# The recurrent layer's input strips computed as high and low parts in three products, with a changed order on VectorE

## The reference

```
xs = proj + (prev - proj) * mu                 # proj = rmsnorm(h) @ rwkv_w_in, 256 x 2816
r, k, v, wl, al, gl = jnp.split(xs, offs, axis=-1)
w = -jax.nn.softplus(-(w0 + jnp.tanh(wl) @ w2)) - 0.5
decay = jnp.exp(-jnp.exp(w.astype(jnp.float32)))
a = jax.nn.sigmoid(a0 + al @ a2)
g = jax.nn.sigmoid(gl) @ g2
kk = (k * k_k).reshape(B, S, H, N).astype(jnp.float32)
kk = kk * lax.rsqrt(jnp.maximum(jnp.sum(kk * kk, axis=-1, keepdims=True), 1e-24))
k = k * (1.0 + (a - 1.0) * k_a)
...
s = jnp.einsum('bshd,bmhd->bhsm', q, mem_k).astype(jnp.float32) * (HEAD_DIM ** -0.5)
p = jax.nn.softmax(s, axis=-1)
```

## Time and profile before

| | us |
|---|---|
| median of 3 runs | 764.37 (762.6 to 765.59) |
| the profiled execution: its own time | 763.08 |
| the profiled execution: span of its trace | 761.4 |
| PE busy in the span | 721.2 (95%) |
| DVE busy | 443.9 (58%) |
| ACT busy | 393.1 (52%) |
| first strip's first matmul to the first chunk matmul | 363.56 to 463.19 |

### The profile page before, as it was taken

How to read it: one execution, slowest core, us unless ns; L and a number is a source line. 1 busy time by engine, 2 the same in 40 slices (tenths; PEclk the granted TensorE clock), 3 DMA queues, 4 the chain that set the end, 5 groups by cost and what they waited for, 6 DMA issues and landing times.

```text
span 761.4 us, 14999 instructions
## 1 busy us (share of the span) xinstructions
PE 721.2 (95%) x6453; PEld 619.7 (81%) x6453; DVE 443.9 (58%) x645; ACT 393.1 (52%) x655; POOL 106.6 (14%) x163
## 2 busy tenths in 40 slices
PE   4999998999999999999999998998799999999997
PEld 4789975688888888888888877997678888888885
DVE  3778787646865675532243547553557757656523
ACT  5744766547655555532465535543258554556311
POOL 8120066700000000000300054700000000000000
PEclk9999989999999999999999999999999999999999
DMA  8846710008665565553844331000028565655511
GB/s 308 314 143 203 268 56 2 2 0 262 209 204 183 185 203 168 218 169 111 278 129 158 111 111 59 4 5 4 3 87 273 183 205 169 207 177 191 196 56 55
DMA packets 78276, 111.70 MB, mean 147 GB/s; under 512 B 2124, under 2 KB 64738, under 8 KB 78210
## 3 DMA queue, kind: packets, MB, share of 16 engines
q1 hardware_dynamic: 77090, 107.67, 42.4%
q0 software_dynamic: 976, 3.04, 1.2%
q10 hardware_dynamic: 144, 0.04, 0.0%
HBM read 109.68 MB, written 1.05 MB: 145 GB/s over the span
## 4 chain that ended last, share of the span: by engine, by line
PE 87%; DVE 5%; ACT 4%; issue 2%; DMA 1%; POOL 0%; DVEq 0%; SPq 0%; ACTq 0%; POOLq 0%
PE ps L1060 20%; PE ps L746 10%; PE ps L748 10%; PE ps L747 10%; PE ps L1063 10%; PE ps L1048 8%; PE ps L1225 5%; PE ps L1235 3%; PE ps L780 2%; PE ps L866 2%; PE ps L889 2%; PE ps L915 2%; DVE w_lo L1895 2%; DMA hn<-mem 1%; ACT w_hi L1422 1%
## 5 line engine op out<-in xcount | busy, mean ns | idle before, releaser
L1895 DVE TENSOR_TENSOR w_lo<-w_raw,w_hi 128x2048 fp32r<-128x2048 f32 (+2 forms) x90 | 202.2, 2260 | 84.5 <-ACT w_hi L1422 84.5
L1060 PE MATMUL ps<-x_hi_lo,w_hi 128*128 128x512 f32 x640 | 201.2, 396 | 0.0
L1422 ACT ACTIVATE w_hi<-w_raw 128x2048 fp32r<-128x2048 f32 (+2 forms) x90 | 168.0, 1886 | 39.6 <-PE ps L748 38.2
L1063 PEld LDWEIGHTS ps<-x_hi_lo,w_lo 128*128 128x128 f32 x640 | 120.2, 188 | 28.4
L1063 PE MATMUL ps<-x_hi_lo,w_lo 128*128 128x256 f32 x640 | 125.7, 278 | 0.0
L1060 PEld LDWEIGHTS ps<-x_hi_lo,w_hi 128*128 128x128 f32 x640 | 97.4, 189 | 0.0
L746 PE MATMUL ps<-w_hi,x_hi_lo 128*128 128x512 f32 (+3 forms) x208 | 74.0, 356 | 5.3 <-DVE x_hi_lo L2123 3.4
L748 PE MATMUL ps<-w_hi,x_hi_lo 128*128 128x512 f32 (+3 forms) x208 | 71.9, 346 | 0.0
L747 PE MATMUL ps<-w_lo,x_hi_lo 128*128 128x512 f32 (+3 forms) x208 | 71.9, 346 | 0.0
L746 PE MATMUL ps<-w_hi,hidden_hi 128*128 128x512 f32 x176 | 68.6, 390 | 0.0
L747 PE MATMUL ps<-w_lo,hidden_hi 128*128 128x512 f32 x176 | 68.5, 389 | 0.0
(11 more groups left out here) (367 smaller groups left out, 984.8 us busy)
## 6 DMA issues: line engine op xcount, KB each, us to landing
w_raw<-w_ffn_in SPq DMA_DIRECT2D x44, 1024.0 KB, 5.1
w_raw<-w_ffn_out SPq DMA_DIRECT2D x22, 1024.0 KB, 4.9
w_raw<-rwkv_w_in SPq DMA_DIRECT2D x11, 1024.0 KB, 5.3
w_raw<-w_out SPq DMA_DIRECT2D x8, 1024.0 KB, 4.9
w_raw<-nsa_w_in SPq DMA_DIRECT2D x6, 1024.0 KB, 14.7
w_raw<-w_mem_kv SPq DMA_DIRECT2D x2, 1024.0 KB, 8.9
w_raw<-nsa_cmp_k_w SPq DMA_DIRECT2D x2, 1024.0 KB, 5.5
w_raw<-nsa_cmp_v_w SPq DMA_DIRECT2D x2, 1024.0 KB, 5.5
```

Of the source, the lines that this page charges most:

```text
L1060: pe.matmul(psum[:, bank + j, :], kt_of(w_hi, i, k)[:, cols[j]], xx[:, k, :, :].rearrange("p c n -> p (c n)"), start=k == 0, stop=False)
L1063: ins = pe.matmul(psum[:, bank + j, 0:SEQ], kt_of(w_lo, i, k)[:, cols[j]], xh[:, k, :], start=False, stop=k == KD - 1)
L1422: act.activation(w_hi[:, i % SPL, 0:size(i)], raw[:, i % RAW, 0:size(i)], ACT.Copy).then_inc(hi_done, 1)
L1895: dve.tensor_tensor(w_lo[:, i % RAW, 0:size(i)], raw[:, i % RAW, 0:size(i)], w_hi[:, i % SPL, 0:size(i)], ALU.subtract).then_inc(lo_done, 1)
```

## The change

All 11 strips are split into high and low parts like every other piece: ACT and DVE each get 11 more instructions of 128x2048, `x_rwkv` goes, and `join(1)` writes `x_hi_lo` as the other joins do. In `feature_strip` and `tok_strip` the one float32 product becomes three of fp32r. Counters that skipped the strips (`whole`, `split_no`) go. On DVE the lower bound of the key norms moves from step 5 to step 4, ahead of that step's `shift`; the scaled `kkT` and `aT` stand ahead of `shift(6)`; `split_to` loses the exception on ACT and on DVE alike; the twelve `a_rT` come in two halves of six around the first row maxima; the bonus terms and the scaled keys come later; ACT makes no split in step 6 and the last one in step 7.

```diff
             def tok_strip(m, t, part, i):
-                if whole(i):
-                    pe.wait_ge(landed[i % RAW], land_value[i])
-                else:
-                    pe.wait_ge(lo_done, split_no(i) + 1)
+                pe.wait_ge(lo_done, i + 1)
                 for k in range(KD):
-                    if whole(i):
-                        if part == 0 and k % 2 == 0:
-                            pe.wait_ge((j_hi, j_lo)[k // 2 % 2], tile_base(m, t) + k // 4 + 1)
-                        ins = pe.matmul(psum[:, turn_bank(m, t) + part, 0:FC], xf[:, k, tile(t)], raw_kt(i, k),
-                                        start=k == 0, stop=k == KD - 1)
-                        continue
...
             def feature_strip(i, bank, between=None):
-                pe.wait_ge(landed[i % RAW], land_value[i])
+                pe.wait_ge(lo_done, i + 1)
                 for j in range(2):
                     c = slice(P * j, P * j + P)
                     for k in range(KD):
-                        ins = pe.matmul(psum[:, bank, j * SEQ:(j + 1) * SEQ], raw_kt(i, k)[:, c], xf[:, k, :],
-                                        start=k == 0, stop=k == KD - 1)
+                        ins = three(psum[:, bank, j * SEQ:(j + 1) * SEQ], kt_of(w_hi, i, k)[:, c], kt_of(w_lo, i, k)[:, c],
+                                    xh[:, k, :], xl[:, k, :], start=k == 0, stop=k == KD - 1)
...
             def split_to(n):
                 for i in range(split[0], min(n, NPIECES)):
-                    if whole(i):
-                        continue
...
-                if 2 <= q <= MQ - 1:
+                if 2 <= q < MQ - 1:
                     split_to(first["rwkv"] + q + 3 + AHEAD)
+                if q == MQ:
+                    split_to(first["rwkv"] + MQ + 2 + AHEAD)
...
-            def rate_factors():
+            def rate_factors(fs):
                 dve.wait_ge(ex_ok, 2)
                 dve.wait_ge(shifted, 7)
-                for f in range(FT):
+                for f in fs:
...
-                split_to(first["rwkv"] + q + 3 + AHEAD)
+                if q < MQ - 1:
+                    split_to(first["rwkv"] + q + 3 + AHEAD)
+                if q == 4:
+                    for j in range(FT // 2):
+                        dve.wait_ge(ss_mm, j + 1)
+                        dve.tensor_scalar(eP_sq[:, 2 * j:2 * j + 2, :], psum[:, j, :].rearrange("p (j n) -> p j n", j=2), 1e-24, None,
+                                          ALU.max).then_inc(ss_ev, 1)
+                if q == 6:
+                    dve.wait_ge(ss_rt, 1)
+                    link(dve.tensor_tensor(kkT[:], kkT[:], eP_sq[:], ALU.mult))
+                    link(dve.tensor_tensor(aT[:], aT[:], kkT[:], ALU.mult))
                 if q not in (0, 3):
                     shift(q)
...
+            rate_factors(range(FT // 2))
             maxima(1, 0)
-            bonus_terms()
+            rate_factors(range(FT // 2, FT))
             maxima(1, 1)
             factors(1, 0)
-            shift(MQ + 1)
-            scaled_keys()
+            split_to(first["rwkv"] + MQ + 2 + AHEAD)
             maxima(1, 2)
             factors(1, 1)
-            shift(MQ + 2)
+            shift(MQ + 1)
+            bonus_terms()
             maxima(1, 3)
             factors(1, 2)
             probs_out(1, 1)
+            shift(MQ + 2)
             factors(1, 3)
+            scaled_keys()
```

More of the change, by code:

```diff
@@ L170, in trunk @@
         xh, xl = xx[:, :, 0, :], xx[:, :, 1, :]
-        xf = at(o_x, "x_rwkv", [P, KD, SEQ])
         o_hn = base[0]
@@ L390, in kt_of @@
             return buf[:, i % (RAW if buf is w_lo else SPL), k * n:(k + 1) * n]
-        N_STRIPS = len(RWKV_ORDER)
-        def whole(i):
-            return first["rwkv"] <= i < first["rwkv"] + N_STRIPS
-        def split_no(i):
-            return i if i < first["rwkv"] else i - N_STRIPS
-        def raw_kt(i, k):
-            n = pieces[i].shape[2]
-            return raw[:, i % RAW, k * n:(k + 1) * n]
         def tile_base(m, t):
-            return (0, 8, 12)[m] + (2 if m == 1 else 4) * t
+            return 4 * (TT * m + t)
         land_value, count = [], [0] * RAW
@@ L1023, in full_gemm @@
                     if t == 0:
-                        pe.wait_ge(lo_done, split_no(i0 + j) + 1)
+                        pe.wait_ge(lo_done, i0 + j + 1)
                         if j < n_ready:
@@ L1275, in _ @@
             pe.wait_ge(bo_ev, 3)
-            pe.wait_ge(ar_ok, 1)
+            pe.wait_ge(ar_ok, 2)
             pe.wait_ge(bk_ok, 1)
@@ L1580, in tile_hi @@
                     col = NORM_COL[m + 2] + k
-                    if m == 1:
-                        if k // 2 % 2 == 0:
-                            ins = act.activation(xf[:, k, tile(t)], quarter(m, t, k), ACT.Copy, scale=colA[:, col:col + 1])
-                            if k % 2:
-                                ins.then_inc(j_hi, 1)
-                        continue
                     ins = act.activation(xh[:, k, tile(t)], quarter(m, t, k), ACT.Copy, scale=colA[:, col:col + 1])
@@ L1891, in split_to @@
                 for i in range(split[0], min(n, NPIECES)):
-                    if whole(i):
-                        continue
-                    dve.wait_ge(hi_done, split_no(i) + 1)
+                    dve.wait_ge(hi_done, i + 1)
                     dve.tensor_tensor(w_lo[:, i % RAW, 0:size(i)], raw[:, i % RAW, 0:size(i)], w_hi[:, i % SPL, 0:size(i)],
@@ L2112, in tile_lo @@
                     col = NORM_COL[m + 2] + k
-                    if m == 1:
-                        if k % 4 == 2:
-                            dve.wait_ge(j_tp, 2 * n + k // 4 + 1)
-                        if k // 2 % 2:
-                            ins = dve.tensor_scalar(xf[:, k, tile(t)], quarter(m, t, k), colA[:, col:col + 1], None, ALU.mult)
-                            if k % 2:
-                                ins.then_inc(j_lo, 1)
-                        continue
                     if k % 2 == 0:
@@ L2284, in bonus_terms @@
             def bonus_terms():
-                dve.wait_ge(ar_ok, 1)
+                dve.wait_ge(ar_ok, 2)
                 for f in range(FT):
@@ L2325, in _ @@
                     link(dve.tensor_tensor(k_T[:].rearrange(flat), vT[:].rearrange(flat), k_T[:].rearrange(flat), ALU.mult))
-                if q == 5:
-                    for j in range(FT // 2):
-                        dve.wait_ge(ss_mm, j + 1)
-                        dve.tensor_scalar(eP_sq[:, 2 * j:2 * j + 2, :], psum[:, j, :].rearrange("p (j n) -> p j n", j=2), 1e-24, None,
-                                          ALU.max).then_inc(ss_ev, 1)
-                if q == 6:
-                    dve.wait_ge(ss_rt, 1)
-                    link(dve.tensor_tensor(kkT[:], kkT[:], eP_sq[:], ALU.mult))
-                    link(dve.tensor_tensor(aT[:], aT[:], kkT[:], ALU.mult))
-                    rate_factors()
+            rate_factors(range(FT // 2))
             maxima(1, 0)
-            bonus_terms()
+            rate_factors(range(FT // 2, FT))
             maxima(1, 1)
             factors(1, 0)
-            shift(MQ + 1)
-            scaled_keys()
+            split_to(first["rwkv"] + MQ + 2 + AHEAD)
             maxima(1, 2)
             factors(1, 1)
-            shift(MQ + 2)
+            shift(MQ + 1)
+            bonus_terms()
             maxima(1, 3)
```

1 line of the change is left out of this document (removed).

## The result

| | us, median | lowest to highest | executions |
|---|---|---|---|
| before | 764.98 | 762.60 to 769.73 | 4 |
| after | 753.09 | 752.75 to 757.05 | 4 |

The ratio is 0.985, with a 95% interval of 0.982 to 0.988. Two later groups gave 0.986 (0.983 to 0.989; 753.94 against 765.27) and 0.986 (0.984 to 0.988; 753.35 against 764.67). The profiled execution of the changed kernel took 752.97 us, with a span of 751.2. The forecast was 755.3, with a range of 752.0 to 760.5.

What follows compares the result with a forecast made beforehand. PE alone was taken to bound the strips. Cheaper products save 12.65 us, less 0.64, 1.4 and 2.3 us at three waits: 8.3 us less, giving 754.8 or 756.1; forecast 755.3 us, range 752.0 to 760.5.

Steps and rivals of the forecast that it cites:

- The product: Each strip's 48 fp32r products start 0.12 us apart: 5.76 us against 6.91, so 12.65 us less for 11 strips.
- rival 5: Weight loads in the strips are not hidden: 9.0 us a strip, 23 us more in all, 786 us; chance 0.04.
- The splits: Low-part splits add 16.7 us on ACT and 20.3 on DVE; they fit in sum, only their queue places cost.
- (b): At `strip_turns(0)`, ACT's copies of strips 0 and 1 stand behind the splits of strips 2 to 4: PE waits 1.4 us.
- (c): Strip 8 needs `strip_out(6)`, last of a long row on ACT (22.8 us): PE waits 2.3 us.
- (a): At the join, PE starts the second token tile 2.05 us after the turns instead of 1.41: 0.64 us given back.
- The margin that I called the thinnest: Before `strip_out(6)`, DVE's lower bound of the norms is ready at 416.4, ACT's table at 416.7: 0.3 us.
- Behind strip 8: Up to the first chunk matmul, moved DVE rows cost nothing; scaled keys are ready 6 us ahead of it.
- The sum: Whole kernel: 12.65 - 0.64 - 1.4 - 2.3 = 8.3 us less, giving 754.8 from the profile, 756.1 from the median.
- The main case: Whole kernel: the forecast itself, 755.3 us, taken as 753.5 to 757.5 us; chance 0.62.
- rival 2: The stalls at strip 0's transposes or at strip 8 do not appear: 752 to 753 us; chance 0.06.
- rival 3: PE's waits let the clock fall to half in the strips, costing 2.5 us or twice that: 757 to 760; chance 0.05.

## Why the prediction was right

**The product.** Forecast 5.76 us a strip, 12.65 for eleven. In the changed kernel gates and two strips take 14.10 us (394.58 to 408.68) where they took 16.40 (397.40 to 413.80): 1.15 a strip. From PE's timeline, after and then before:

```profile
394.58 2.75 PE L1160 MATMUL ps<-lora_in,gate_w 128*128 128x256 f32 x12
...
408.68 2.75 PE L1169 MATMUL ps<-kk_squares,head_blocks 128*128 128x256 f32 x12
```
```profile
413.80 2.75 PE L1191 MATMUL ps<-kk_squares,head_blocks 128*128 128x256 f32 x12
```

The 48 products of the first token tile take 5.76 us (363.43 to 369.19), as forecast. They start 0.12 us apart on both sides of the exchange of weights and activations. The timeline of weight loads within strip 4:

```profile
399.92 0.19 PEld L733 LDWEIGHTS ps<-x_hi_lo,w_hi 128*128 128x128 f32 x1
400.04 0.19 PEld L734 LDWEIGHTS ps<-x_hi_lo,w_hi 128*128 128x128 f32 x1
400.16 0.19 PEld L735 LDWEIGHTS ps<-x_hi_lo,w_lo 128*128 128x128 f32 x1
```

A load of 0.19 us starts every 0.12, as in the earlier trace rows, so rival 5 is out. The Trainium skill (TensorE: Matmul & The Clock Gate, The mechanism) has in its list that loads overlap running matmuls only where row groups differ; this trace does not agree, all 128 rows being the same. The text above that list also lets a load go ahead into the background weight buffer, and no run here shows whether that is the way these loads take. The Trainium skill (FP8 and Floating Point Precision, TensorE Precision Notes) counts four passes for true float32; the estimate from it, 5.2 us a strip for three passes, was not measured either.

**The splits.** Forecast: hidden in sum, with a cost only by their places. The kernel with all splits and one float32 product shows the first half: ratio 1.000. Under the faster products the places cost the 1.06 and 1.50 us of (b) and (c).

**(a) The join.** Forecast 2.05 us from the turns to the second tile's start; measured 2.05 (369.19 to 371.24).

**(b) Strip 0's transposes.** Forecast a wait of 1.4 us; measured 1.06. The mechanism is the forecast one, as its removal by the copies' place shows. ACT's three splits ran from 371.84 to 377.4 as counted, and PE could start 0.37 us sooner than I had it: 0.16 because the splits began at 371.84 and not at 372.0, the rest because the copies overlap (four in 1.25 us). ACT's timeline:

```profile
371.84 5.57 ACT L1398 ACTIVATE w_hi<-w_raw 128x2048 fp32r<-128x2048 f32 x3
377.25 1.25 ACT L1675 ACTIVATE strip_tok<-ps 128x256 f32<-128x256 f32 x4
```

**(c) Strip 8.** Forecast 2.3 us; measured 1.50. PE's arrival was right (423.0, measured 422.93), and so was the length of ACT's row: 22.8 us counted, 22.55 measured (401.63 to 424.18). What was mis-sized was its start. I had the scans 0.5 us earlier than before, at 391.5; they began at 390.38, 5.85 us behind strip 1's transposes (384.53) as before (386.20 to 392.05). I had moved the transposes and not carried their whole gain to the scans. So `kkT` was ready at 401.6, not 402.6. The row then ended at 424.18 and PE began 0.26 us later. DVE's timeline, then ACT's:

```profile
390.38 3.89 DVE L2284 TENSOR_TENSOR_SCAN decay_sums<-consts,log_decay 128x128 f32<-128x128 f32 x12 [2.92 <-ACT log_decay L1725]
...
399.93 1.67 DVE L2264 TENSOR_SCALAR kkT<-kT_rwkv,cols_b 128x256 f32<-128x256 f32 x6
```
```profile
401.63 1.49 ACT L1740 ACTIVATE kk_squares<-kkT 128x1536 f32<-128x1536 f32 x1 [2.59 <-DVE kkT L2264]
...
423.70 0.48 ACT L1695 ACTIVATE rT<-ps,one_minus_mu_ka 128x256 f32<-128x256 f32 x1
```

The margin that I called the thinnest, 0.3 us between the norms' bound and ACT's table, came out at 0.43, with ACT the later of the two, and the old order shows what lies behind it: 4.8 us.

**Behind strip 8.** Forecast: nothing. Between 424.44 and 453.70 PE waits 0.29 us for `probsT`, as before, and 1.09 for its own issue. The last of the scaled keys ends at 447.9, 5.8 us ahead of the chunk; 6 were forecast.

**The sum.** By the measured terms it is 12.65 - 0.64 - 1.06 - 1.50 = 9.45, and the distance shrank by 9.36, where 8.3 was forecast. So the size of two waits, 1.14 us together, is what the forecast missed in this stretch. The profiled executions differ by 10.1 us, the medians by 11.9, 11.3 and 11.3. Of what the 10.1 have beyond 9.36, 0.1 lies ahead of the join and 0.7 behind the first chunk matmul: 298.2 us to the end of the span before, 297.5 after. The stretch 540 to 545 ran at 0.66 of the clock before, and none there was low after:

```profile
540.00:545.00 5.00, 4.40 (x71) 3.84 (x66) 1.29 (x4) 1.09 (x3) 0.00 (x0) 0.66 0.02 3
```

That is one execution of each. In the two later profiles of the changed kernel the clock did fall there. What is between 10.1 and the 11.3 to 11.9 of the medians is not shown by any run: the profiled execution of before lay 1.9 us under the median of its group, that of after at its median. The part behind the first chunk matmul took 298.2, 299.8 and 300.7 us in the three kernels with float32 strips and 296.5 to 298.7 in the ten profiles with three products and the new order; a part of the gain may lie there. Against the products as its cause stands the kernel with three products and the old order, where it took 300.9. The cause stays open. PE's waits for its own issue in this part sum to 6.6 to 8.3 us in these four profiles and to 4.9 to 7.0 in the ten others; the two ranges overlap, so this settles nothing.

The point forecast, 755.3 us, was 2.2 us too high: 1.1 for the stretch, nearly all of it the two waits, and as much for what lies outside of it. The gain that was added up, 8.3 us, was 3 us short of the medians' 11.3 to 11.9, and only these 1.1 us of it have a shown cause. The main case had 753.5 to 757.5 us; 753.09 lies just under it, beside the 752 to 753 of rival 2. That is no success of rival 2 as it was put, that (b) or (c) does not appear: both appeared, with 1.06 us for 1.4 and 1.50 for 2.3. So the mechanism and its places were forecast rightly; that the total lies inside the range owes something to the range's width, since some 2 us of the gain come from where nothing was forecast.

## What to carry to other kernels

Price an exchange of products by the distance between the starts of the same product elsewhere in the trace, and then follow the queues of the engines that feed it, name by name: here the products' gain of 12.65 us was lost whole under the old order of two other engines. Where a wait hangs on a row of work of one engine, count all that stands ahead of the read that ends it, and look for a second link that is ready at the same time; two level links must be moved together, and each alone shows little (here 0.02 and 0.42 us of 1.71).

## What was not expected of the hardware

The clock fell inside the strips, behind long waits of PE. In the kernel with the old order PE had no matmul from 424.90 to 431.17 us. Stretches of it (columns as in the earlier trace rows):

```profile
425.00:430.00 5.00, 0.00 (x0) 0.00 (x0) 0.00 (x0) 4.99 (x6) 0.00 (x0) 0.94 0.67 213
430.00:435.00 5.00, 3.83 (x18) 3.86 (x19) 2.25 (x2) 3.21 (x5) 0.00 (x0) 0.50 0.00 0
435.00:440.00 5.00, 5.00 (x36) 4.54 (x35) 4.93 (x7) 0.00 (x0) 0.00 (x0) 0.88 0.01 3
...
450.00:455.00 5.00, 2.74 (x17) 2.75 (x18) 2.47 (x5) 2.48 (x8) 4.03 (x4) 0.83 0.61 209
455.00:460.00 5.00, 4.35 (x32) 3.84 (x31) 2.07 (x6) 1.51 (x5) 2.38 (x3) 0.83 0.02 3
```

From 430 to 435 the granted clock is 0.50, that is 1.2 instead of 2.4 GHz, and the first 24 products of strip 8 take 5.35 us, from the start of the first to the end of the last record, where they take 3.10 in the changed kernel. Around the 2.70 us wait it is 0.83, and the 24 products behind it take 4.60 us instead of 3.11. That is 2.25 and 1.5 us, 3.7 together, on top of the waits themselves. Behind the single waits of 1.0 to 1.5 us in the changed kernel the clock stayed at 1.00, so the mechanism of rival 3 exists in this stage, and the waits of the changed kernel did not bring it about. The wait of 6.28 us thus cost 2.25 us more than its length, which a sum of queues does not count. All this is from one execution of that kernel.
